# More projection units of three mixers computed as split products, and the transposes of the feed-forward norm moved inside a unit

## The reference

```
A  attention (stick-breaking and banded)   w_in 1024 x 3072   out 1024 x 1024
FFN 0  silu(h @ gate) * (h @ up) @ down    1024 x 2816
R  gated linear recurrence with convolution w_in 1024 x 2048
FFN 1
E  dilated and differential attention       w_in 1024 x 3072
FFN 2
G  HGRN2: q, forget, value, output gate     w_in 1024 x 4096
M  mixture of eight experts, top two        3584 wide each
```

## Time and profile before

| | |
|---|---|
| median of 3 runs | 2092.36 us (2090.61 to 2092.63) |
| time of the profiled execution | 2093.63 us |
| its span on the core | 2091.7 us |
| PE, DVE, ACT busy share of the span | 99%, 68%, 58% |
| granted clock of PE over the span | 0.998 |
| E from its first unit to the end of its attention | 609 to 731 us |
| G from its first unit to its output matrix | 947 to 1084 us |
| experts | 1130 us to the end |

### The profile page before, as it was taken

How to read it: one execution, slowest core, us unless ns; L and a number is a source line. 1 busy time by engine, 2 the same in 40 slices (tenths; PEclk the granted TensorE clock), 3 DMA queues, 4 the chain that set the end, 5 groups by cost and what they waited for, 6 DMA issues and landing times.

```text
span 2091.7 us, 26804 instructions
## 1 busy us (share of the span) xinstructions
PE 2065.4 (99%) x10550; PEld 1712.9 (82%) x10550; DVE 1429.7 (68%) x1174; ACT 1210.6 (58%) x1117; POOL 79.0 (4%) x142
## 2 busy tenths in 40 slices
PE   9989999999999999999999999999999999999998
PEld 9858889788898668889877888888888888888877
DVE  3755446664436645443646889888888888888797
ACT  3654434653425634333545777786777778777674
POOL 1000000100000000000002100000000000000100
PEclk9999999999999999999999999999999999999999
DMA  8427655566645246645426999999999999999997
GB/s 284 136 86 261 222 184 161 182 212 228 204 149 161 81 141 233 220 161 178 132 85 235 410 368 398 365 394 375 383 378 374 389 363 397 372 389 377 379 402 281
DMA packets 211788, 561.23 MB, mean 268 GB/s; under 512 B 10557, under 2 KB 67998, under 8 KB 211566
## 3 DMA queue, kind: packets, MB, share of 16 engines
q1 hardware_dynamic: 204224, 530.61, 70.1%
q0 software_dynamic: 5552, 28.84, 3.4%
q10 hardware_dynamic: 1934, 0.67, 0.1%
HBM read 553.27 MB, written 16.25 MB: 272 GB/s over the span
## 4 chain that ended last, share of the span: by engine, by line
PE 93%; DVE 3%; ACT 2%; DMA 1%; issue 1%; POOL 0%; DVEq 0%; ACTq 0%; SPq 0%
PE ps L2218 14%; PE ps L2220 14%; PE ps L2219 14%; PE ps L538 9%; PE ps L667 5%; PE ps L669 5%; PE ps L668 5%; PE ps L631 3%; PE ps L708 3%; PE ps L710 3%; PE ps L709 3%; PE ps L570 3%; PE ps L2271 1%; PE ps L694 1%; DMA ring<-in_moe_w_gate 1%
## 5 line engine op out<-in xcount | busy, mean ns | idle before, releaser
L2214 DVE TENSOR_TENSOR ring_r<-ring,ring_r 128x2048 fp32r<-128x2048 f32 x336 | 752.4, 2286 | 103.0 <-ACT ring_r L2209 102.8
L2209 ACT ACTIVATE ring_r<-ring 128x2048 fp32r<-128x2048 f32 x336 | 627.1, 1913 | 68.6 <-DMA ring<-in_moe_w_gate 50.9
L2218 PE MATMUL ps<-ring_r,arena_r 128*128 128x512 f32 x1344 | 530.5, 395 | 1.0 <-DVE arena_r L2472 1.0
L2220 PE MATMUL ps<-ring_r,arena_r 128*128 128x512 f32 x1344 | 524.2, 390 | 0.0
L2219 PE MATMUL ps<-ring_r,arena_r 128*128 128x512 f32 x1344 | 524.0, 390 | 0.0
L340 DVE TENSOR_TENSOR ring_r<-ring,ring_r 128x2048 fp32r<-128x2048 f32 x119 | 272.2, 2291 | 219.4 <-ACT ring_r L331 219.3
L331 ACT ACTIVATE ring_r<-ring 128x2048 fp32r<-128x2048 f32 x119 | 227.4, 1914 | 188.3 <-DMA ring<-in_ffn_w_up 78.2
L2220 PEld LDWEIGHTS ps<-ring_r,arena_r 128*128 128x128 f32 x1344 | 252.6, 188 | 54.0
L2218 PEld LDWEIGHTS ps<-ring_r,arena_r 128*128 128x128 f32 x1344 | 252.8, 188 | 52.4 <-issue 1.2
L2219 PEld LDWEIGHTS ps<-ring_r,arena_r 128*128 128x128 f32 x1344 | 253.0, 188 | 50.7
L667 PE MATMUL ps<-ring_r,arena_r 128*128 128x512 f32 (+1 forms) x576 | 216.0, 375 | 4.7 <-DVE arena_r L452 2.7
(11 more groups left out here) (394 smaller groups left out, 1986.6 us busy)
## 6 DMA issues: line engine op xcount, KB each, us to landing
ring<-in_moe_w_gate SPq DMA_DIRECT2D x115, 1024.0 KB, 5.6
ring<-in_moe_w_up SPq DMA_DIRECT2D x112, 1024.0 KB, 6.2
ring<-in_moe_w_down SPq DMA_DIRECT2D x112, 1024.0 KB, 5.5
ring<-in_ffn_w_gate SPq DMA_DIRECT2D x33, 1024.0 KB, 5.1
ring<-in_ffn_w_up SPq DMA_DIRECT2D x33, 1024.0 KB, 5.1
ring<-in_ffn_w_down SPq DMA_DIRECT2D x33, 1024.0 KB, 5.0
ring<-in_attn_w_in SPq DMA_DIRECT2D x24, 1024.0 KB, 5.7
ring<-in_hgrn_w_in SPq DMA_DIRECT2D x16, 1024.0 KB, 5.5
```

The lines of the kernel that those rows point to most:

```text
L2209: nc.scalar.activation(unit_parts(k)[0], ring[:, slot_of(k), 0:2048], ACT.Copy).then_inc(m_hi, 1)
L2214: nc.vector.tensor_tensor(low, ring[:, slot_of(k), 0:2048], high, ALU.subtract).then_inc(m_lo, 1)
L2218: nc.tensor.matmul(out_, x[:, 0, f, :], w[0], start=first, stop=False)
L2220: return nc.tensor.matmul(out_, x[:, 0, f, :], w[1], start=False, stop=last)
```

## The change

Of each mixer that splits tokens, three first units stay raw instead of four. Split in addition are unit 3 of A, units 3 to 7 of E and units 3, 4, 5, 6, 8, 12, 13, 14, 15 of G. E and G get split tokens of their own. In E four reciprocals on DVE become a logarithm and an exponential on ACT. In G the sums over time are interleaved with the exponents. In the feed-forward networks that follow a mixer with a norm behind it (FFN 0 and 1), the transposes of tile 1 go into the middle of unit `up[0, 1]`, and in FFN 0 one high part is made earlier.

```
-        A_plan = project(..., tuple(range(4, 12)))
+        A_plan = project(..., tuple(range(3, 12)))
-        E_plan = project(E_w_in, ...)
+        E_plan = project(E_w_in, ..., (3, 4, 5, 6, 7))
-        G_plan = project(G_w_in, ...)
+        G_plan = project(G_w_in, ..., (3, 4, 5, 6, 8, 12, 13, 14, 15))
...
 ffn_norm_scalar:
-                highs_to(act, first + 1)
+                highs_to(act, first + (2 if k == 1 else 1))
...
 ffn_tensor:
-                up_tokens(0, 1, 0)
+                tokens(up[0, 1], 2, 0, 1, 0, 0)
                 norm_turn(pe, k, 1)
+                tokens(up[0, 1], 2, 0, 1, 0, 1).then_inc(s_u, 1)
...
 A_tensor:
-            first_tokens(pe, 0, first_units(A_plan, 4))
+            first_tokens(pe, 0, first_units(A_plan, 3))
+            pe.wait_ge(s_ol, split_at["A tokens"])
+            half(3, 0)
+            half(3, 1)
             setup_tensor(pe)
+            pe.wait_ge(s_ol, split_at["A tokens"] + 1)
...
 E_tensor:
-            half(4, 0), sum_squares(0)
-            half(4, 1), sum_squares(1)
-            half(5, 0), sum_squares(2)
-            half(5, 1), sum_squares(3)
+            pe.wait_ge(s_ol, split_at["E tokens"])
+            half(3, None)
+            half(4, 0), sum_squares(0), sum_squares(1)
+            half(4, 1)
+            half(5, 0), sum_squares(2), sum_squares(3)
+            half(5, 1)
...
 E_scalar:
+            nc.scalar.activation(E_tokens[0], HTf, ACT.Copy).then_inc(s_oh, 1)
+            highs_to(act, E_plan[4][1])
+            def inverse_roots(*of):
+                for i in of:
+                    act.wait_ge(e_nn, i + 1)
+                    nc.scalar.activation(E_rs[:, i, :], ps[:, mean_bank(i), :], ACT.Ln, ...).then_inc(e_rt, 1)
+                for i in of:
+                    act.wait_ge(e_rt, i + 1)
+                    nc.scalar.activation(E_rs[:, i, :], E_rs[:, i, :], ACT.Exp, scale=-0.5).then_inc(e_inv, 1)
-            for j in range(4):
-                evac(j)
-            root(0), root(1)
+            evac(0), evac(1)
+            highs_to(act, E_plan[5][1])
+            evac(2)
+            highs_to(act, E_plan[6][1])
+            evac(3)
+            inverse_roots(0, 1)
             evac(4)
-            root(2)
+            highs_to(act, E_plan[7][1])
+            inverse_roots(2, 3)
             evac(5)
-            root(3)
...
 E_vector:
+            nc.vector.tensor_tensor(E_tokens[1], HTf, E_tokens[0], ALU.subtract).then_inc(s_ol, 1)
+            lows_to(dve, E_plan[6][1])
-            normalise(0), normalise(1), normalise(2)
+            normalise(0), normalise(1)
+            lows_to(dve, E_plan[7][1])
+            normalise(2)
...
 G_scalar: the tokens' high part and high parts 3, 4 ahead of the first unit's evacuation;
           5 and 6 behind the evacuations of units 1 and 2; 8 behind the third exponential;
+                    if 4 <= i < 8:
+                        highs_to(act, G_plan[8 + i][1])
 G_vector: the tokens' low part and low parts 3, 4 ahead; 5, 6 behind the first passes over
           logits 1 and 3; 8 ahead of the sums over time;
+            sums_over_time(0)
+            sums_over_time(1)
             exponents(0)
+            sums_over_time(2)
+            sums_over_time(3)
+            products(0)
             exponents(1)
-            products(0)
...
+                if 4 <= i < 8:
+                    lows_to(dve, G_plan[8 + i][1])
```

More of the change, by code:

```diff
@@ L209, in build @@
                         ("G out", 2)):
-            if part not in unsplit:
-                split_at[part] = count + 1
-                count += n
+            split_at[part] = count + 1
+            count += n
         s_g = sem("s_g")
@@ L288, in build @@
         A_plan = project(A_w_in, [(c, "F") for c in (1536, 2048, 1792, 2304)] + several("H", 2560, 2)
-                         + [(c, "F") for c in (0, 512, 256, 768)] + several("H", 1024, 2), tuple(range(4, 12)))
+                         + [(c, "F") for c in (0, 512, 256, 768)] + several("H", 1024, 2), tuple(range(3, 12)))
         A_out = project_out(a["attn_w_out"][0], (2, 3, 0, 1), raw=2)
@@ L658, in ffn_tensor, with tokens @@
             last = CHUNKS_FF - 1
-            def tokens(u, bank, c, h, t):
+            def tokens(u, bank, c, h, t, part=None):
                 weights_ready(pe, u)
@@ L664, in tokens @@
                 o = ps[:, bank + t, 0:w]
-                for kt in range(rows_):
+                for kt in range(rows_) if part is None else (2 * part, 2 * part + 1):
                     k = rows_ * h + kt
@@ L975, in half @@
             def half(j, part):
-                unit_tensor(pe, A_plan, j, A_banks, part, (HTh, A_lows[j > 4]))
+                unit_tensor(pe, A_plan, j, A_banks, part, (HTh, A_lows[j > 3]))
             def scores(m):
@@ L1165, in A_vector @@
             nc.vector.tensor_tensor(A_lows[0], HTf, HTh, ALU.subtract).then_inc(s_ol, 1)
+            unit_low(3)
+            dve.wait_ge(*used(A_plan[2][1]))
+            nc.vector.tensor_tensor(A_lows[1], HTf, HTh, ALU.subtract).then_inc(s_ol, 1)
             unit_low(4)
@@ L1832, in E_vector @@
             lows_to(dve, E_out[3][0] + 1)
-        G_q, G_k, G_b, G_g, G_o = (tiles(i) for i in (3, 4, 5, 7, 3))
+        G_q, G_k, G_b, G_g, G_o = (tiles(i) for i in (3, 4, 5, 1, 3))
         G_v = page(6).rearrange("p (t d) -> p t d", t=TT)
@@ L1862, in G_tensor @@
         def G_tensor(pe):
-            first_tokens(pe, 6, first_units(G_plan, 4))
+            first_tokens(pe, 6, first_units(G_plan, 3))
             def half(j, part=None):
-                unit_tensor(pe, G_plan, j, G_banks, part)
+                unit_tensor(pe, G_plan, j, G_banks, part, G_tokens)
             def scores(h):
@@ L1919, in sum_squares @@
                 nc.tensor.matmul(ps[:, G_norm_bank[u], :], ones128[:, :], G_sq[:, u, :], start=True, stop=True).then_inc(g_nn, 1)
-            for j in range(4, 9):
+            pe.wait_ge(s_ol, split_at["G tokens"])
+            for j in range(3, 9):
                 half(j)
@@ L1943, in G_scalar @@
             norm_scalar(act, 6)
+            act.wait_ge(s_hth, 4 * 6 + 4)
+            act.wait_ge(s_htl, 4 * 6 + 4)
+            nc.scalar.activation(G_tokens[0], HTf, ACT.Copy).then_inc(s_oh, 1)
+            highs_to(act, G_plan[4][1])
             for u in range(4):
                 unit_scalar(act, G_plan, u, G_banks, G_b[:, 2 * u:2 * u + 2, :])
+                if u in (1, 2):
+                    highs_to(act, G_plan[u + 4][1])
             for u in range(4):
@@ L2031, in G_vector @@
             norm_vector(dve, 6)
+            dve.wait_ge(s_oh, split_at["G tokens"])
+            nc.vector.tensor_tensor(G_tokens[1], HTf, G_tokens[0], ALU.subtract).then_inc(s_ol, 1)
+            lows_to(dve, G_plan[4][1])
             for u in range(4):
@@ L2048, in G_vector, with sums_over_time @@
                 nc.vector.tensor_tensor(ls, ls, f2, ALU.subtract).then_inc(g_kk, 1)
-            for u in range(4):
+            lows_to(dve, G_plan[8][1])
+            def sums_over_time(u):
                 mx, ad = G_mx[:, u, :], G_ad[:, u, :]
```

43 lines of the change are left out of this document (26 added, 17 removed).

## The result

The changed kernel takes **2071.98 us** in the median of 4 runs (2070.79 to 2073.72), against 2091.49 us for the kernel before on the same chip (4 runs, 2090.45 to 2092.63). The ratio is 0.9906, 95% interval 0.9891 to 0.9921: faster by 19.5 us. Run once more beside other kernels, it took 2072.29 us (4 runs) against 2092.16 us: 0.9901, 0.9886 to 0.9916. The forecast was 2075.8 us, its range 2073.2 to 2081.5 us.

The account below looks back on a forecast made before the run. PE, busy 99% of the span, was taken as the bound; gains of 1.2 (A), 2.0 (FFN 0), 0.85 (FFN 1), 5.0 (E) and 7.5 (G) make 16.6 us, so 2092.4 - 16.6 = 2075.8 us, range 2073.2 to 2081.5.

Parts of the forecast that it names:

- the price on PE: On PE, a split unit costs 5.94 us, so converting a later unit gains 0.96 us, a first unit about 1.26.
- the second tile's transposes: In E, tile 1's transposes come before their input is complete, so PE loses 0.2 us.
- The slack of 0.9 us: In G before the first scores, PE's way still outlasts the path through `products(0)` by 0.9 us.
- the start of the loop: At the start of G's loop over heads, `products(1)` comes later and PE loses 0.25 us.
- the third output unit: In G, its low part doesn't move with unit 15, so 0.75 to 0.8 us become a PE wait.
- Low 12: In G's loop, unit 12's low part is ready at 1044.5, wanted at 1044.33; 0.25 us lost.
- (c): Whole kernel: nothing waits, giving 2074.2 us or a little less; chance 0.08.
- (a): E and G: more waits than counted, gain 9 to 14 us, time 2078.4 to 2083.4; chance 0.24.
- (d): E and G: ACT and DVE set the pace, PE's saving becomes waits, 4 us gained, 2088.4; chance 0.05.
- (b): E: table switches with a drain make ACT stand, leaving E 1 us gain, 2079.8 us; chance 0.03.
- (e): G and E: late loads for high parts hold up evacuations; slower than before from landings of 17 to 18 us; chance 0.03.
- Four passes: Split units on PE: by the skill's rule a unit falls from 6.90 to 5.2 us, time about 2065 us.

Follow-up runs that it names:

- G alone: The kernel before with only the change's part in mixer G (units 3 to 6, 8 and 12 to 15 split): 2081.80 us, ratio 0.9945.
- E alone: The kernel before with only the change's part in mixer E (three raw first units, units 3 to 7 split, new roots): 2085.75 us, ratio 0.9963.

## Why the prediction was right or wrong

**The step that failed** is the price on PE: "A split unit ran from 48.08 to 54.02 with nothing between, 5.94 us ... So a converted later unit gives 0.96 us, a converted first unit 7.2 - 5.94 = about 1.26 us." The mechanism was right, the term was too small. A unit in a row costs 5.75 us, which makes 6.90 - 5.75 = 1.15 and 7.15 - 5.75 = 1.40; an interrupted one gives 1.18 to 1.20 (the period in G, and unit 7 of E). I had subtracted a split unit with the changes at its ends from a raw unit at the price of a row. The forecast of 2.97 us for an interrupted split half held: one takes 2.94 us, from 1034.05 to 1036.99. For 3 first and 12 later units that is 3 x 0.14 + 12 x 0.19 to 0.23, 2.7 to 3.2 us, more than the 2.1 us by which the stages passed the sum; the rest went back into waits. The same step set the range: its lowest case, "nothing waits" at 2074.2 us, was built on 0.96 and 1.26.

**Point by point.** A: 1.41 for 1.2, the price alone. FFN 0: 2.08 for 2.0. FFN 1: 0.63 to 0.81 for 0.85. E: 5.81 for 5.0, and unit 7 done 58.0 us after E's start for 58.6; by the new prices 1.40 + 4 x 1.15 = 6.0, less 0.2 us at the second tile's transposes, as I had it (they take 1.28 us instead of 1.03). G to its first `scores`: 67.52 us before, 61.53 after, 5.99 gained for 4.75, which is 1.40 + 4 x 1.15 with no wait at all. The slack of 0.9 us that I gave PE's way there was 0.4 (`products(0)` ends at 997.99, PE begins at 998.44), and unit 7 in the split set used it up. From there to the end of G 2.8 us for 2.8, and that this agrees is luck: the larger price went into waits that were larger too, 0.5 for 0.25 at the start of the loop and, with all that it cost, 1.10 for 0.77 at the third output unit. Low 12 was ready at 1028.57 and PE began at 1028.63, so that wait is 0.1 at most.

**Rivals.** (c), nothing waits, was nearest by its time, but by luck, since its mechanism didn't occur: the waits came, and units that were cheaper than thought made up for them. (a) expected more waits than came, (d) fell with G alone and E alone, which gave all they had. (b) fell with the rows of the table loads, and the run with the old roots turned it over: fewer loads, 1.4 us longer. (e) never came near: in G ACT waited 1.3 and 1.4 us for the loads of units 5 and 6, and held up nothing that PE needed.

**Four passes.** By the rule of the Trainium skill, page "FP8 and Floating Point Precision", section "TensorE Precision Notes", that true float32 takes four passes through the array, I had estimated that a unit would fall from 6.90 to 5.2 us and the time be about 2065. The trace has 5.75, a ratio of 0.83 and not 0.75, and the measured time is 7 us above that case. A quarter of one of the 16 float32 products of a raw unit is 6.90 / 64 = 0.108 us, and an fp32r product takes 0.12. The estimate had taken the two as equal; over 48 products the difference is the 0.6 us that it lacked.

**What was in no term.** Between the sum over the stages, 18.7, and 19.5 to 19.9 in the medians lie 0.35 us of a shorter wait at the routing, seen in every profile with G's part, some 0.2 us around the span (1.9 in the kernel before, 1.5 to 1.8 after), and a rest of 0.2 to 0.6. The clock's falls have at most a small share in the medians. Runs with the same clock can be compared: at a mean clock of 0.999 or more the spans of the changed kernel (5 runs) lie 19.3 us under those of the kernel before (19 runs), at 0.998 or less 19.3 as well (3 against 23). That longer idle time makes the fall longer is shown by the run without filling, all five of which have a low clock. Whether G's part made it rarer at the gather isn't shown: with 8 filling products the clock was down there in three of four profiles without this part and in none of seven with it, which is one or two executions of each kernel. Why DVE comes to the routing 0.35 us sooner stays open: its gap of 1.33 us ahead of that step became 0.98, with the same instructions around it. The profiled span of before, at 2091.7 us, was one of its slower executions; the 22.1 us between the two profiles overstate the change by about 2.5.

## What to carry to other kernels

When one form of an operation replaces another, price both in the same surroundings: both in a row, or both between the same neighbours. A row from one place against a row from another put 0.2 us on each of 15 units. Parts that are made on other engines are worth the saving only where both fit beside PE's work: one more unit in G cost 2.25 us, though it takes 1.15 from PE, and moving two calls by a few instructions brought 1.1. Before the gain of a small change is believed, compare the granted clock in the same stretch of both profiles, also in stages that it doesn't touch.

## What the runs showed of the hardware

- Products of fp32r with 256 columns follow each other in 0.12 us, 48 of them in 5.75 us. Between float32 products a split unit takes 5.94 us, some 0.1 more at each end; a raw half between the small products of G takes 3.50 us instead of 3.45.
- PE's clock fell to 0.50 behind idle times of 0.87 and 1.1 us in a stretch with little work, in some executions and not in others of one kernel, and at the waits of 1.6 and 0.75 us at the start of FFN 0 in three of the profiles. Without the filling products it fell in the idle time of 2.4 us in the profile, and all five runs had a low mean clock. Once down, it stayed for 3.4 to 6.8 us behind the short waits and for nearly 14 with the long one.
- The cost of such a fall is small where PE waits anyway: nothing in FFN 0 with G alone, where a wait of 1.57 us took it up, and 0.55 us in the changed kernel, where that wait was 0.32. It is larger where PE computes: about 2.1 us in the profiled execution of before, against the profile with 11 filling products at the full clock (1.1 in the routing, 1.1 in the experts). Without the filling products, whose results nothing uses, the median was 4.2 us longer.
